# Splitting the attention output into its high and low parts as it is made, instead of in the retention stage

## The reference

```python
h = rmsnorm(x, g_pre[l]) * (1.0 + scale) + shift
proj = h @ w_in[l]
y_mla = mla_branch(...)            # 8 heads, causal softmax attention, 128 values a head
y_mla = y_mla * jax.nn.silu(gate_mla)
y_ret = retention_branch(...) * jax.nn.silu(gate_ret)   # 4 heads, chunks of 128 tokens
merged = (jax.nn.sigmoid(merge_mla) * (y_mla @ w_proj_mla[l])
          + jax.nn.sigmoid(merge_ret) * (y_ret @ w_proj_ret[l]))
x = x + gate * (merged @ w_out[l])
return rmsnorm(x, g_final)
```

## Time and profile before

| | us |
|---|---|
| median of 3 runs | 1633.92 |
| lowest, highest | 1633.48, 1634.14 |
| the profiled execution's own time | 1633.92 |
| its span, first to last instruction | 1632.1 |
| mean granted PE clock | 0.994 of full |

### The profile page before, as it was taken

How to read it: one execution, slowest core, us unless ns; L and a number is a source line. 1 busy time by engine, 2 the same in 40 slices (tenths; PEclk the granted TensorE clock), 3 DMA queues, 4 the chain that set the end, 5 groups by cost and what they waited for, 6 DMA issues and landing times.

```text
span 1632.1 us, 20172 instructions
## 1 busy us (share of the span) xinstructions
PE 1588.2 (97%) x7724; PEld 1328.4 (81%) x7724; DVE 969.9 (59%) x1512; ACT 580.4 (36%) x984; POOL 234.8 (14%) x180
## 2 busy tenths in 40 slices
PE   5999999999999999999999999999999999999998
PEld 4778888888888888888888878888788888888886
DVE  6984444444447857556666555566856665547544
ACT  5444333333334323332343333334533333213111
POOL 2232223222211212112000000010201000000000
PEclk8999999999999999999999999999999999999999
DMA  9132222232241577777554554547977877335332
GB/s 387 32 129 107 110 110 110 107 124 107 107 141 41 162 278 248 292 272 262 199 191 171 168 203 156 193 155 260 359 217 240 254 232 269 131 123 199 135 104 78
DMA packets 150993, 292.33 MB, mean 179 GB/s; under 512 B 10737, under 2 KB 91505, under 8 KB 142961
## 3 DMA queue, kind: packets, MB, share of 16 engines
q1 hardware_dynamic: 132816, 253.47, 44.9%
q10 hardware_dynamic: 13472, 20.78, 3.9%
q0 software_dynamic: 4608, 16.78, 2.6%
HBM read 187.71 MB, written 102.76 MB: 178 GB/s over the span
## 4 chain that ended last, share of the span: by engine, by line
PE 85%; DVE 8%; DMA 3%; ACT 2%; issue 1%; POOL 0%; SPq 0%; DVEq 0%; ACTq 0%
PE p_banks L2044 9%; PE p_banks L2002 8%; PE p_banks L2005 8%; PE p_banks L2004 8%; PE p_banks L2076 5%; PE p_banks L1917 5%; PE p_banks L1919 5%; PE p_banks L1918 5%; PE p_banks L2251 4%; PE p_banks L2252 4%; PE p_banks L2253 4%; DMA w_raw<-in_w_dense 2%; PE p_banks L2312 2%; PE p_banks L2310 2%; PE p_banks L2311 2%; PE p_banks L2143 2%
## 5 line engine op out<-in xcount | busy, mean ns | idle before, releaser
L1517 DVE TENSOR_TENSOR w_form<-w_pair,w_form 128x512 fp32r<-128x512 f32 x120 | 92.9, 776 | 101.8 <-ACT w_form L1171 100.5
L1171 ACT ACTIVATE w_form<-w_pair 128x512 fp32r<-128x512 f32 x120 | 75.6, 632 | 195.3 <-PE p_banks L2005 187.3
L518 ACT ACTIVATE w_hi<-w_raw 128x1024 fp32r<-128x1024 f32 (+3 forms) x79 | 70.1, 890 | 209.7 <-PE p_banks L2253 100.4
L1917 PE MATMUL p_banks<-h_hi,w_hi 128*128 128x512 f32 x304 | 118.6, 390 | 1.7 <-DVE w_lo L524 1.6
L1919 PE MATMUL p_banks<-h_hi,w_lo 128*128 128x512 f32 x304 | 118.3, 389 | 0.0
L1918 PE MATMUL p_banks<-h_lo,w_hi 128*128 128x512 f32 x304 | 118.3, 389 | 0.0
L524 DVE TENSOR_TENSOR w_lo<-w_raw,w_hi 128x1024 fp32r<-128x1024 f32 (+3 forms) x80 | 91.9, 1153 | 30.4 <-ACT w_hi L518 30.1
L1241 ACT ACTIVATE prob<-p_banks,neg_max 128x128 f32<-128x128 f32 (+3 forms) x64 | 47.5, 742 | 163.8 <-DVE neg_max L1620 163.8
L2253 PE MATMUL p_banks<-y_hi,w_lo 128*128 128x512 f32 x256 | 99.6, 389 | 0.0
L2252 PE MATMUL p_banks<-y_lo,w_hi 128*128 128x512 f32 x256 | 99.6, 389 | 0.0
L2251 PE MATMUL p_banks<-y_hi,w_hi 128*128 128x512 f32 x256 | 99.6, 389 | 0.0
(11 more groups left out here) (291 smaller groups left out, 4271.8 us busy)
## 6 DMA issues: line engine op xcount, KB each, us to landing
w_raw<-in_w_dense SPq DMA_DIRECT2D x45, 512.0 KB, 5.4
w_pair<-in_w_pairs SPq DMA_DIRECT2D x20, 1024.0 KB, 4.8
v_ret<-v_stage POOLq DMA_DIRECT2D x32, 512.0 KB, 3.9
qk_chunk<-qk_chunks SPq DMA_DIRECT2D x32, 512.0 KB, 4.2
v_chunk<-v_ret SPq DMA_DIRECT2D x32, 512.0 KB, 5.2
qk_chunks<-split_stage SPq DMA_DIRECT2D x28, 512.0 KB, 6.0
merge_t<-act_t SPq DMA_DIRECT2D x48, 256.0 KB, 3.5
act_t<-stage SPq DMA_DIRECT2D x40, 256.0 KB, 2.0
```

What stands on the lines that cost most here:

```text
L1517: nc.vector.tensor_tensor(self.form[f % FORM_SLOTS][:, 1, :], self.form_source(f), self.form[f % FORM_SLOTS][:, 0, :].bitcast(F32), ALU.su ...
L1917: nc.tensor.matmul(out, w_hi[:, slot, cut], x_hi[:, k, tok], start=(k == ks[0]), stop=False)
```

## The change

The split of the attention output into its pair moves from retention into attention, and three things move with it.

- In every even step of attention ACT now rounds the 128x256 piece (`y_pair[.., 0, :]`) and DVE takes the rest (`y_pair[.., 1, :]`), and SP stores both (256 KB in place of 128 KB) to `y_hl`. `y_full` moves to another address.
- In retention the heads of set 0 come as two 512 KB loads each, straight into `y_hi` and `y_lo`. The eight ACT and eight DVE instructions for them are gone. The loads of heads 5 to 7 come later (`SET0_LOAD`), and the third merge weight is split in step 6, not 7.
- The twelve weight parts of the fill are issued by POOL, not SP, with a semaphore of their own.
- The values of heads 1 to 7 are issued by SP, not ACT.

```diff
-MERGE_SPLIT = (2, 5, 7)
-SET0_LOAD = {2: (2, 3), 3: (4, 5), 4: (6, 7)}
-SET0_SPLIT = {0: (0,), 1: (1,), 3: (2,), 4: (3, 4), 5: (5,), 6: (6, 7)}
+MERGE_SPLIT = (2, 5, 6)
+SET0_LOAD = {2: (2, 3), 3: (4,), 4: (5,), 5: (6,), 6: (7,)}
...
-        self.y_full = z("y_full", 96, [P, 2, 256])
+        self.y_full = z("y_full", 38, [P, 2, 256])
+        self.y_pair = z("y_pair", 96, [P, 2, 2, 256], F32R)
...
+    def weight_loaded(self, r):
+
+        late = (V_GROUPS - 1) * V_PARTS
+        if R_MERGE - late <= r < R_MERGE:
+            return self.v_part_loaded, 16 * (r - R_MERGE + late + 1)
+        return self.w_loaded[r % RING], 16 * (r // RING + 1 - (late // RING if r >= R_MERGE else 0))
...
@@ sync_attention
+            if i == 2 and 1 <= h < H_MLA:
+                self.load_v(sp, h)
...
-            while parts < self.parts_used(g - 2):
-                if parts + 1 < (V_GROUPS - 1) * V_PARTS:
-                    self.load_weight(sp, R_V + V_PARTS + parts + 1)
-                parts += 1
...
-                sp.wait_ge(self.y_done, pair + 1)
-                sp.dma_start(d["y_mla"][head][:, 256 * q:256 * q + 256], self.y_full[:, pair % 2, :])\
+                sp.wait_ge(self.y_lo_ready, pair + 1)
+                sp.dma_start(d["y_hl"][head][:, :, 256 * q:256 * q + 256], self.y_pair[:, pair % 2, :, :].bitcast(F32))\
@@ load_set0
-        sp.dma_start(self.y_raw[k][:, :], self.d["y_mla"][k]).then_inc(self.set_loaded[k], 16)
+        sp.dma_start(self.y_hi[k][:, :].bitcast(F32), self.d["y_hl"][k][:, 0, :]).then_inc(self.set_loaded[k], 16)
+        sp.dma_start(self.y_lo[k][:, :].bitcast(F32), self.d["y_hl"][k][:, 1, :]).then_inc(self.set_loaded[k], 16)
@@ gpsimd
+            while parts < self.parts_used(g - 2):
+                if parts + 1 < (V_GROUPS - 1) * V_PARTS:
+                    self.load_weight(pool, R_V + V_PARTS + parts + 1)
+                parts += 1
@@ scalar_attention
-            if g % NT == 2 and NT < g < STEPS:
-                self.load_v(act, g // NT)
...
+            if g >= 4 and g % 2 == 0:
+                pair = (g - 4) // 2
+                act.wait_ge(self.y_done, pair + 1)
+                if pair == 0:
+                    act.wait_ge(self.v_stored[2], 16)
+                if pair >= 2:
+                    act.wait_ge(self.y_stored[pair % 2], 16 * (pair // 2))
+                nc.scalar.activation(self.y_pair[:, pair % 2, 0, :], self.y_full[:, pair % 2, :], ACT.Copy)\
+                    .then_inc(self.y_hi_ready, 1)
@@ scalar_retention, vector_retention
-            for k in SET0_SPLIT.get(n, ()):
-                self.split_set(act, 0, k)
@@ vector_attention
+            if g >= 4 and g % 2 == 0:
+                dve.wait_ge(self.y_hi_ready, pair + 1)
+                nc.vector.tensor_tensor(self.y_pair[:, pair % 2, 1, :], self.y_full[:, pair % 2, :],
+                                        self.y_pair[:, pair % 2, 0, :].bitcast(F32), ALU.subtract)\
+                    .then_inc(self.y_lo_ready, 1)
@@ fill_set
-                pe.wait_ge(self.set_lo_ready, k + 1)
+                pe.wait_ge(self.set_loaded[k], 32)
```

More of the change, by code:

```diff
@@ L283, in semaphores @@
         self.tables_stored = sem("ret_tables_stored")
[L284 removed]
+        self.tables_loaded = sem("k_pe_swapped_and_tables_loaded")
         self.consts_split = sem("consts_split")
@@ L302, in semaphores @@
         self.total_rounded = sem("latent_total_rounded")
-        self.swapped = sem("k_pe_swapped")
+        self.v_part_loaded = sem("v_weight_part_loaded")
         self.roped = sem("k_pe_roped")
@@ L334, in semaphores @@
         self.y_done = sem("y_done")
+        self.y_hi_ready = sem("y_pair_hi_ready")
+        self.y_lo_ready = sem("y_pair_lo_ready")
         self.y_stored = [sem("y_even_stored"), sem("y_odd_stored")]
@@ L497, in load_weight @@
             queue.wait_ge(*self.part_free(V_GROUPS - 1, 0))
-        queue.dma_start(self.raw_place(r), self.weight(r)[0]).then_inc(self.w_loaded[r % RING], 16)
+        queue.dma_start(self.raw_place(r), self.weight(r)[0]).then_inc(self.weight_loaded(r)[0], 16)
     def split_weight(self, act, r):
@@ L502, in split_weight @@
             return
-        act.wait_ge(self.w_loaded[r % RING], 16 * (r // RING + 1))
+        act.wait_ge(*self.weight_loaded(r))
         group, part = divmod(r - R_V, V_PARTS)
@@ L1000, in gpsimd @@
                 nc.gpsimd.tensor_tensor(rot[:, 3, :], rot[:, 3, :], rot[:, 1, :], ALU.add).then_inc(self.rot_added, 1)
-        units = 0
+        self.load_weight(pool, R_V + V_PARTS)
+        units = parts = 0
         for g in range(STEPS + 4):
@@ L1320, in split_set @@
         i = z_set * KD + k
-        if z_set < 2:
-            act.wait_ge(self.set_loaded[k], 16 * (z_set + 1))
+        if z_set == 1:
+            act.wait_ge(self.set_loaded[k], 48)
         else:
             act.wait_ge(self.set2_loaded, 16 * KD)
-        scale = self.t["cols"][:, COL_GRET + i - KD:COL_GRET + i - KD + 1] if z_set else 1.0
-        self.nc.scalar.activation(self.y_hi[i][:, :], self.y_raw[i][:, :], ACT.Copy, scale=scale)\
+        self.nc.scalar.activation(self.y_hi[i][:, :], self.y_raw[i][:, :], ACT.Copy,
+                                  scale=self.t["cols"][:, COL_GRET + i - KD:COL_GRET + i - KD + 1])\
             .then_inc(self.set_hi_ready, 1)
     def split_out_weight(self, act, k):
-        act.wait_ge(self.set_loaded[k], 48)
+        act.wait_ge(self.set_loaded[k], 64)
         self.nc.scalar.activation(self.out_hi[k][:, :], self.out_raw[k][:, :], ACT.Copy).then_inc(self.out_hi_ready, 1)
@@ L1401, in rot_products @@
         if (kind, i) == ("x", 0):
-            dve.wait_ge(self.tables_loaded, 16)
+            dve.wait_ge(self.tables_loaded, 64 + 16)
         elif first:
@@ L1628, in vector_attention @@
                 if pair >= 2:
-                    dve.wait_ge(self.y_stored[pair % 2], 16 * (pair // 2))
-                elif pair == 0:
-                    dve.wait_ge(self.v_stored[2], 16)
+                    dve.wait_ge(self.y_lo_ready, pair - 1)
                 nc.vector.tensor_tensor(self.y_full[:, pair % 2, :], p[:, 0, 0:256],
@@ L1752, in lower_set @@
         i = z_set * KD + k
[L1753 to L1757, removed]
+        dve.wait_ge(self.set_hi_ready, i - KD + 1)
         self.nc.vector.scalar_tensor_tensor(out=self.y_lo[i][:, :], in0=self.y_raw[i][:, :],
@@ L2096, in scores @@
                 pe.wait_ge(self.late_loaded, 48)
-                pe.wait_ge(self.tables_loaded, 32)
+                pe.wait_ge(self.tables_loaded, 64 + 32)
             q = slice(i * P, (i + 1) * P)
@@ L2262, in tensor_merge @@
         for k in range(KD):
-            pe.wait_ge(self.set_lo_ready, KD + k + 1)
+            pe.wait_ge(self.set_lo_ready, k + 1)
             for unit in range(2 * KD, 2 * KD + 4):
@@ L2277, in tensor_merge @@
             if tile == 2 * KD:
-                pe.wait_ge(self.set_lo_ready, 3 * KD)
+                pe.wait_ge(self.set_lo_ready, 2 * KD)
             if tile == SETS * KD - 2:
@@ L2351, in build @@
             "k_rope": scratch("k_rope", (P, 2, S)),
-            "y_mla": scratch("y_mla", (H_MLA, P, S)),
+            "y_hl": scratch("y_hl", (H_MLA, P, 2, S)),
             "y_ret": scratch("y_ret", (H_RET * 4, P, S)),
```

8 lines of the change are left out of this document (2 added, 6 removed).

## The result

The kernel after takes **1655.84 us** in the median of 4 runs, against 1633.90 us before: ratio 1.0143, 95% interval 1.0129 to 1.0157. It is slower, as forecast, but by 22 us where 6.5 were forecast, and outside the range (1631 to 1648). The ratio rests on 20 executions with a median of 1656.9; single executions that took far longer (one of the four here, 1699 us, and one of e7's five, 3228 us) are in the medians and not in the ratios. The profiled execution took 1658.31 us, with a span of 1656.5 (before 1632.1): 24.4 us to explain.

The account below looks back on a forecast made before the run. PE was taken to bound the kernel, busy 1588.2 of 1632.1 us, so only its standstills could move. 1633.92 + 5.3 (bytes) + 1.6 (pieces) - 0.4 (values) = 1640.4 us, range 1631 to 1648.

Parts of the forecast that it names:

- Weight parts on POOL ... I take 0: Attention: issuing the fill's weight parts from POOL costs nothing; bounds -3.6 to +3.6 us.
- The Trainium skill's figure against this edit: Attention: GpSimd's slower first byte would make four weight parts on POOL cost +1.6 us, an estimate not taken into the sum.
- 5.3 us of bytes ahead of the fourth weight: Retention: doubled set 0 loads make the fourth merge weight land later, +5.3 us; bounds 0 and +12.9.
- Its issue does not move: Retention: SP issues the fourth merge weight when chunk buffers come free, which PE decides, so its issue time stays.
- The forecast's sign for itself: Retention: the fourth merge weight landing more than 9 us after its issue would show the forecast right.
- Head 7's own landing, hidden: Retention step 7: PE waits some 3 us for head 7's pair, hidden before its later transposes; 0, upper end +4.
- a hole of 8.6 us at `out_n`: Retention: PE's hole before the transposes of step 8 grows from 3.3 to 8.6 us.
- The clock, 0: Retention, behind the hole: the stretch at half clock does not lengthen; 0, upper end +2.5 us.
- Pieces, +1.6: Attention: added ACT and DVE pieces show only where PE waits for the exponential, +1.6 us; bounds 0 and 3.2.
- v_head on SP, -0.4: Attention: values issued earlier by SP remove PE's one wait for them, -0.4 us; bounds -1.4 and 0.
- Relief by 16 fewer splits, 0: Retention, 1120 to 1168 us: dropping eight ACT and eight DVE instructions is worth 0, as PE has no hole there.
- The rival of 1646 us: Retention: SP's full queue, late third weight, head 7's wait and longer slow clock cost 5.8 us above the forecast; chance 0.18.

Follow-up runs that it names:

- e7: Kernel after with weight parts issued by SP and v_head loads by ACT again, output pieces and doubled set loads kept; 1644.56 us, ratio 1.0049.
- e2: Kernel before with only the twelve weight parts issued by POOL; splits, v_head and retention as before; 1644.70 us, ratio 1.0065.
- e12: Kernel after with SP's q and k loads of heads 5 and 7 waiting until the weight part beside them has landed; 1641.93 us, ratio 1.0039.
- e5: Kernel before with each of the eight set 0 loads made twice (4.19 MB more traffic), all splits kept; 1642.13 us, ratio 1.0046.
- e13: As e12, with the fourth merge weight loaded one retention step earlier (step 6, not 7); 1640.44 us, ratio 1.0032.
- e4: Kernel before with the fourth merge weight loaded in retention step 6, not 7; 1633.18 us, ratio 0.9986; measured again with more rounds, 1631.48 us, 0.9978.
- e1: Kernel after with the twelve weight parts issued by SP again, v_head left on SP, all else as changed; 1646.69 us, ratio 1.0071.
- e10: As e7, with the fourth merge weight loaded one retention step earlier (step 6, not 7); 1640.22 us, ratio 1.0032.
- e14: As e13, with sets 2 to 7 of the merge each loaded one retention step earlier; 1636.72 us, ratio 1.0004.

## Why the prediction was wrong

- *"Weight parts on POOL ... I take 0"*, bounds of 3.6 us either way: **the step that failed**. I priced a part by the median landing of its queue, 3.2 against 4.1 us, and the median did stay (4.3). What changed is what stood ahead of it. On one queue the parts that ACT needed at once were in front of q and k, because SP waited with them; on two queues q and k run off first, and two parts of eleven landed in 9.5 and 10.4 us. e2 (the move alone: +13.4 us in attention) and e12 (the order restored, the queue kept: 17.4 falls to 2.9) show it from both sides. The order in `sync_attention` would have told it: whatever SP waits for also holds back what is behind. And the median of 3.2 us hid the price: six of those 25 stores by GpSimd were issued within 5 us behind a head's k, and they landed after 8.2 to 10.4 us.
- *The Trainium skill's figure against this edit* (first byte after about 1 us from GpSimd, 0.6 from sync) pointed the right way and not at the cause. The part at 1043.84 us is issued 0.28 us after its weight was lowered (1042.33 + 1.23), SP did so in 0.02 (1038.19 + 1.23, then 1039.44); the median landings are 4.3 and 4.1 us. That is half a microsecond a part, and e12 keeps it.
- *5.3 us of bytes ahead of the fourth weight, "if SP's transfers are served in their order"*: more bytes do make the weight late and PE wait, and the size holds (e5: 5.3 us in the trace; 7.0 in the kernel after). How they make it late was wrong, and is the next point.
- *"Its issue does not move"*: wrong. SP's issues were held by the full queue for up to 4.82 us and the weight was issued 6.2 us late. It counts mostly instead of the longer landing, not on top: 8.26 us landing, not 6.4 + 5.3. The forecast's sign for itself, a landing of more than 9 us, did not come.
- *Head 7's own landing, hidden*: nearly, but not behind a hole of 8.6 us at `out_n`. PE waited 5.3 us for `y_lo`, 2.1 of it up to 1188 and 3.2 up to 1195 us, and so only 2.7 us were left to wait for `out_n`. The chain ran through the weight all the same; in e13, where the weight no longer hides it, this wait is what is left.
- *The clock, 0*: too low. PE's granted clock is 0.51 in 1190 to 1200 us, and each lump in attention is followed by a stretch at 1.2 GHz (clock 0.83 in 960 to 980 and in 1040 to 1060 us). A hole of 5 to 8 us is paid once more in part behind it: 5.3 us of attention's 17.2 and 2.4 of retention's 7.0 are not time in which PE stood still. e4 shows it the other way round, 4.3 us gained in the trace by waits 1.8 us shorter.
- *Pieces, +1.6*: not seen. A piece takes ACT 0.41 and DVE 0.42 us, the 0.8 of the forecast, but e7's attention grows no more than an untouched one. What remains of e12's attention is the first lump, 3 us by step 16, which the kernel after has too: there ACT waits 2.5 us for a part and PE 2.2 for the exponential behind it. e7 hasn't got it, nor has e2 (parts on GpSimd, v_head on ACT), nor e1 (parts and v_head on SP). So neither move makes it alone; that it takes the two together is likely, but they were not tried without the pieces.
- *v_head on SP, -0.4*: in the kernel after, where nothing stood ahead of it, PE's wait for `v_head` (0.4 us before) is gone, too little to be seen in a time. e1 shows the sign turn with one instruction ahead of it.
- *Relief by 16 fewer splits, 0*: right; no trace shows a gain.
- The rival of 1646 us named the full queue of retention, but had nothing for attention, and so fell 10 us short as well.

## What to carry to other kernels

When a load is moved to another queue, do not compare the queues' medians (look at the longest landings, and what stood ahead of them): list what its old queue held back behind it, and look at what now starts beside it at the one or two places where its consumer has no slack. A wait in a program is also an order of priority; if the wait moves away, put the order back by a semaphore. Where the DMA engines stood at 1.0 for several steps, an earlier start helped here and a new order within the stretch little (e10 and e13 against e14): it mostly changed what PE waited for.

## What the runs showed of the hardware

- A later transfer on GpSimd's queue got no even share beside q and k on SP's: 0.5 MB landed after all of the 2 MB of q and k, issued up to 1.5 us earlier in one place and up to 4.3 in the other. The Trainium skill, page "DMA: Bandwidth & Descriptors", section "Queues, rings and completion order", says that each engine goes round the queues packet by packet. By even halves at the 391 GB/s of the earlier trace rows the part would have had its 0.524 MB after 2.7 us instead of 1.3, and landed in 5.4 us instead of 4.1, an estimate; the trace shows 10.4. But beside the 1 MB of `v_head` the trace does agree: a part issued 0.24 us behind it, at 862.34, landed in 5.2 us and ahead of it. What makes q and k different stays open. That both queues run on the same 16 engines, as the page's section "Issuing engines are not separate DMA queues" says, the trace bears out: `v_head` took 7.3 us beside that part and 5.9 alone.
- The DMA engines moved 395 GB/s in 1190 to 1200 us at a share of 1.04, and about 360 over the 60 us from 1125 in e13.
- Five issues on SP in the kernel after held its sequencer for 2.1 to 4.8 us, each with 2.5 to 3.75 MB issued and not yet landed, at a DMA share of 1.01 to 1.04; most others take 0.33 to 0.6.
